# A two-block transformer kernel: eleven input panels of each layer of the second block move to split products, their rounded halves in a second ring place

## The chip, the cores and the metric

The kernel runs on one core of a Trainium2 chip. The metric is device time of one launch in microseconds (us), the median of several runs.

## The reference, cut to what matters

Two blocks of two layers each work on 256 tokens of width 1024, all in float32. The change touches only the second block, and in it the first matrix product of each layer:

```python
def second_block(x, c, ...):
    for l in range(DEPTH):                       # 2 layers
        ...
        hn = adaln(x, mix_norm_g[l], sh_m, sc_m)
        (a_q, a_k, a_v, b_qd, b_kvd, b_kr, c_q, c_k, c_v,
         c_qi, c_ki, c_wi, d_q, d_k, d_v) = jnp.split(hn @ w_in[l], IN_SPLITS, axis=-1)
        o_a = diff_attention(...)                # a_q, a_k, a_v
        o_b = latent_attention(...)              # b_qd, b_kvd, b_kr
        o_c = indexed_sparse_attention(...)      # c_*: scores of an index pick the keys
        o_d = chunk_band_attention(...)          # d_q, d_k, d_v
        y = jnp.concatenate([o_a, o_b, o_c, o_d], axis=-1) @ w_out[l]
        x = x + g_m[:, None, :] * y
        ...                                      # layer 0: a dense MLP; layer 1: 8 experts
```

## The kernel before, in words

The program is written out by hand, one instruction stream for each engine; the streams meet at semaphores. What stands first in a stream runs first, and a waiting instruction holds everything behind it on its engine.

**The ring.** All weights come through a ring of six places in on-chip memory, `ring[n % 6]`, one panel of 128x2048 floats (1 MB) in each. SyncE loads panel n when the panel that stood in its place, n-6, has been released by TensorE (`load`, L3060 in the trace). `RING_LOW`, `XT_LOW`, `GATE_HIGH`, `TAB_HIGH` and `PARTS` are not memory of their own: they lie over `ring`, `XT`, `GATE`, `TAB` and the work tiles, as another type (fp32r). So a low half is written in place, over the number that it comes from.

**Two kinds of product.** A plain panel (`panel_T` L664, `panel_tok` L675) multiplies float32 by float32, 16 matmuls, which the trace shows as 32 records. A split panel (`parted_panel`, L719) first has its weights cut in two: ScalarE copies each half of the panel as fp32r, rounded, into an area of its own (`weights_high`), VectorE subtracts it from the panel in place (`weights_low`, L2164), and TensorE forms three products for each plain one: high x high, low x high, high x low, 48 matmuls. The first block, the MLPs and the experts already work so. All 13 input panels of a layer of the second block are plain.

**A layer of the second block before its attention** (keys `s0`, `s1`; L1429 to L1471). TensorE takes panel `c_kw` (`quarters`, L736), then `c_qi`, the small `c_ki` (L1442, L743), a `take` (L634), `b_qd`, a `take`, half of the index scores of token tile 0 (L1428), `b_kvd` (160 columns wide), the other half, `a_q`, a `take` (L630, layer 0 only), half of the index scores of tile 1, `a_k`, a `take`, the other half, the transposes of the latent (L1464, L1468), `a_v`. ScalarE evacuates PSUM (L1599), applies the ReLU to the index scores (L2097) and squares the latent; VectorE sums the index scores by head (`index_sum`, L2902 and L2904) and scales the latent.

**The attention** (`paired_attention`) walks 16 units in pairs. In pass q TensorE transposes the probabilities of units 2q-4 and 2q-3 (L798), forms the scores of units 2q and 2q+1 (L812), does what is hung beside these units, and mixes the values of the two old ones (L832). Beside units 0, 1, 3, 4, 5 and 6 hang the six late panels: `LATE = {0: "d_q", 1: "d_k", 3: "d_v", 4: "c_q", 5: "c_k", 6: "c_v"}`. VectorE finds the maximum of each unit (L2246, L2250), and beside units 0, 1, 3 and 4 searches the top 64 of the index scores (L2301, L2302). ScalarE's stream for step s is, in this order: the exponential of unit s (L1685), the panels of `AHEAD` (none here), the evacuation of the late panel of unit s, and from s = 2 on the copy of the turned probabilities of unit s-2 (`turned`, L1599). GpSimd does nothing in these layers but issue four loads at the start of each.

Of the kernel before, what the change touches and what calls it, by code (L numbers as in the profile page):

```python
# [28 lines left out]
ALU = mybir.AluOpType  # L29
# [3 lines left out]
P = 128  # L33
T = 256
# [5 lines left out]
RING = 6  # L40
# [94 lines left out]
def build_program(nc, d, out):  # L135

    with ExitStack() as ctx:
# [64 lines left out]

        X_HIGH, O_HIGH, OT_LOW = [part_tile(2048 * x) for x in range(3)]
# [153 lines left out]

        weights = {}
# [20 lines left out]
        SPLIT_NORMS = ("mem", "xat0", "xat1")  # L379

# [134 lines left out]
        def part_of(n, what, c, k, i=0):  # L515
# [13 lines left out]
            return REGION_OF[u], pos, i * 16 + 16 * (pos // RING + 1), i * 12 + (made + count)  # L529
# [32 lines left out]
        LATE = {0: "d_q", 1: "d_k", 3: "d_v", 4: "c_q", 5: "c_k", 6: "c_v"}  # L562
# [12 lines left out]
        def _(pe):  # L575
# [63 lines left out]
            def panel():  # L639

                n = state["panel"]
                state["panel"] += 1
                pe.wait_ge(landed[n % RING], 16 * (n // RING + 1))
                return n, ring[n % RING]
# [37 lines left out]
            def part(name):  # L682
# [4 lines left out]
                for area in AREAS[name]:  # L687
                    held.append((area, area_holds.get(area)))
                    area_holds[area] = len(half_done)
                    half_done.append(None)  # L690
# [3 lines left out]
            def half_ready(name, half):  # L694

                n, first, held = weights[name]
                pe.wait_ge(sem("weights_low"), first + half + 1)
                return HALF[held[half][0]], RING_LOW[n % RING][:, 1024 * half:1024 * half + 1024]
# [211 lines left out]
            def late(key, s):  # L910
# [15 lines left out]
                if s in LATE:  # L926
                    name = (key, LATE[s])
                    if LATE[s][-1] == "v":
                        panel_tok(name, bank=bank)
                    else:  # L930
                        panel_T(name, bank=bank)
# [485 lines left out]
            for layer in range(2):  # L1417
# [21 lines left out]
                panel_T((k2, "c_qi"))  # L1439
# [5 lines left out]
                panel_tok((k2, "b_qd"))  # L1445
# [3 lines left out]
                panel_tok((k2, "b_kvd"), w=160)  # L1449
                index_scores(0, (2, 3))  # L1450
                panel_T((k2, "a_q"))
                if layer == 0:
                    take(16, 5)
                index_scores(1, (0, 1))
                panel_T((k2, "a_k"))
                if layer == 0:
                    take(17, 4)
                index_scores(1, (2, 3))
# [11 lines left out]
                panel_tok((k2, "a_v"), bank=7)  # L1470
# [116 lines left out]
        def moe_slot(what, it):  # L1587

            q = moe_plan["p0"] + moe_panel(what, it)
            return q % RING, 16 * (q // RING + 1)  # L1590
# [5 lines left out]
        def _(act):  # L1596
# [245 lines left out]
            def experts():  # L1842
# [73 lines left out]
                for q in range(RING):  # L1916
                    slot = (moe_plan["p0"] + q) % RING
                    act.wait_ge(landed[slot], rounds * (NE * 16 * EPANELS // RING) + 16 * ((moe_plan["p0"] + q) // RING + 1))
# [179 lines left out]

# [1141 lines left out]
```

## Time and profile before

| | us |
|---|---|
| median of 3 runs (2552.0 to 2556.07) | 2554.63 |
| the profiled execution, its own time | 2552.4 |
| its span | 2550.6 |
| TensorE busy | 2474.7 (97%) |
| VectorE busy | 1798.2 (70%) |
| ScalarE busy | 1428.3 (56%) |
| GpSimd busy | 28.7 (1%) |

Starts in the timeline are us from the start of the span. PE is TensorE's matmuls, PEld its weight loads, DVE VectorE, ACT ScalarE, POOL GpSimd, SP SyncE. "[2.72 <-ACT ...]" at a row's end is the idle time of that engine just before it and who ended it. The second block's layer 0 has its input panels and attention from 951 to 1124, layer 1 from 1331 to 1505; between them lies a dense MLP, behind them the experts.

### The profile page before, as it was taken

What the parts mean: (1) busy time and instruction counts of PE and PEld (TensorE: products, weight loads), DVE (VectorE), ACT (ScalarE), POOL (GpSimd) and SP (SyncE); (2) the same over time, 40 slices, a digit from 0 to 9 for tenths busy, and PEclk for the clock granted to TensorE, in tenths of its full rate; (3) what the DMA queues carried; (4) which work ended last, traced back from release to release, by engine and by line L of the source; (5) the groups of instructions that cost most, each with busy time, mean ns of one, the idle gap of its engine ahead of it and who ended that gap; (6) DMA issues with size and microseconds to landing.
All of it is one profiled execution on the core that took longest, in us unless ns stands there. A gap on an engine that the chain in (4) does not pass through costs nothing.

```text
span 2550.6 us, 41384 instructions
## 1 busy us (share of the span) xinstructions
PE 2474.7 (97%) x14738; PEld 2096.1 (82%) x14738; DVE 1798.2 (70%) x2631; ACT 1428.3 (56%) x2078; POOL 28.7 (1%) x41
## 2 busy tenths in 40 slices
PE   7999999998999999999999989999999999999997
PEld 7798998997889988759988757888888888888886
DVE  4654876564648763746544749898989898989897
ACT  5544544423445442444332447777778787877775
POOL 0200000000000000000000000000000000000000
PEclk9999999999999999999999999999999999999999
DMA  7554555323656555236554148898999898989897
GB/s 301 195 202 164 233 197 192 126 83 129 219 200 242 196 203 204 83 112 251 197 200 157 67 157 348 343 359 337 362 340 359 332 373 322 376 326 376 320 379 274
DMA packets 87867, 627.37 MB, mean 246 GB/s; under 512 B 9792, under 2 KB 9952, under 8 KB 13024
## 3 DMA queue, kind: packets, MB, share of 16 engines
q1 hardware_dynamic: 84512, 613.45, 63.7%
q0 software_dynamic: 2704, 11.25, 1.2%
q8 instruction: 66, 1.08, 0.2%
q10 hardware_dynamic: 560, 1.38, 0.1%
q14 instruction: 25, 0.20, 0.0%
HBM read 624.99 MB, written 1.05 MB: 245 GB/s over the span
## 4 chain that ended last, share of the span: by engine, by line
PE 91%; DVE 4%; ACT 2%; issue 1%; DMA 1%; DVEq 0%; SPq 0%; ACTq 0%
PE bank L1156 24%; PE bank L1048 13%; PE bank L1184 12%; PE bank L1062 7%; PE bank L664 7%; PE bank L719 6%; PE bank L983 6%; PE bank L675 4%; PE bank L1267 2%; PE bank L1199 1%; PE bank L1126 1%; PE bank L1171 1%; PE bank L617 1%; PE bank L832 1%; DVE sb_ringlow L2164 1%
## 5 line engine op out<-in xcount | busy, mean ns | idle before, releaser
L1599 ACT ACTIVATE sb_parts<-sb_ring 128x1024 fp32r<-128x1024 f32 x922 | 922.5, 1054 | 99.7 <-PE bank L1184 38.9
L2485 DVE TENSOR_TENSOR sb_parts<-sb_ring,sb_parts 128x1024 fp32r<-128x1024 f32 x675 | 786.4, 1217 | 9.2 <-ACT sb_parts L1599 9.2
L1156 PE MATMUL bank<-sb_parts 128*128 128x512 f32 x2688 | 661.5, 396 | 1.7 <-DVE sb_parts L2477 1.7
L1156 PEld LDWEIGHTS bank<-sb_parts 128*128 128x128 f32 x2688 | 494.9, 188 | 112.6 <-issue 8.6
L1048 PEld LDWEIGHTS bank<-sb_parts 128*128 128x128 f32 x3168 | 384.2, 192 | 9.3 <-DVE sb_parts L2388 3.7
L1048 PE MATMUL bank<-sb_parts 128*128 128x256 f32 x3168 | 386.8, 283 | 4.6 <-DVE sb_parts L2388 2.9
L1184 PE MATMUL bank<-sb_parts 128*128 128x512 f32 x1344 | 323.8, 390 | 0.0
L1184 PEld LDWEIGHTS bank<-sb_parts 128*128 128x128 f32 x1344 | 251.7, 188 | 52.0
L2388 DVE TENSOR_TENSOR sb_parts<-sb_ring,sb_parts 128x1024 fp32r<-128x1024 f32 x198 | 232.6, 1219 | 37.8 <-ACT sb_parts L1599 37.8
L1599 ACT ACTIVATE sb_REG<-bank 128x512 f32<-128x512 f32 (+3 forms) x121 | 68.8, 575 | 231.3 <-PE bank L719 60.7
L1062 PE MATMUL bank<-sb_parts 128*128 128x512 f32 x792 | 185.3, 390 | 0.0
L664 PE MATMUL bank<-sb_XT,sb_ring 128*128 128x256 f32 x768 | 170.9, 383 | 0.0
L1062 PEld LDWEIGHTS bank<-sb_parts 128*128 128x128 f32 x792 | 146.6, 188 | 29.4 <-DVE sb_parts L2388 0.3
L664 PEld LDWEIGHTS bank<-sb_XT,sb_ring 128*128 128x128 f32 x768 | 145.5, 191 | 23.0 <-issue 3.7
L1599 ACT ACTIVATE sb_parts<-bank 128x256 fp32r<-128x256 f32 (+1 forms) x142 | 59.8, 428 | 136.9 <-PE bank L1171 112.4
L2499 DVE TENSOR_TENSOR sb_parts<-bank,sb_parts 128x256 fp32r<-128x256 f32 x112 | 47.3, 423 | 76.1 <-ACT sb_parts L1599 76.1
L675 PE MATMUL bank<-sb_ring,sb_XT 128*128 128x256 f32 (+1 forms) x448 | 94.6, 369 | 1.7 <-ACT sb_XH L1599 1.7
L2427 DVE SCALAR_TENSOR_TENSOR sb_REG<-bank,sb_COL,sb_REG 128x255 f32<-128x255 f32 x88 | 42.4, 482 | 74.8 <-ACT sb_REG L1600 69.1
L1685 ACT ACTIVATE sb_REG<-sb_REG,sb_small 128x256 f32<-128x256 f32 x112 | 55.9, 500 | 65.1 <-DVE sb_small L2250 65.1
L675 PEld LDWEIGHTS bank<-sb_ring,sb_XT 128*128 128x128 f32 x448 | 80.8, 190 | 13.9 <-issue 4.6
L1600 ACT ACTIVATE sb_REG<-bank,sb_COL 128x256 f32<-128x256 f32 x92 | 38.4, 469 | 94.0 <-PE bank L1048 94.0
L1862 ACT ACTIVATE sb_REG<-bank 128x256 f32<-128x256 f32 x112 | 43.3, 387 | 78.7 <-PE bank L1156 76.8
(395 smaller groups left out, 2793.1 us busy)
## 6 DMA issues: line engine op xcount, KB each, us to landing
sb_ring<-in_moe_panels SPq DMA_DIRECT2D x342, 1024.0 KB, 4.9
sb_ring<-in_ada_w SPq DMA_DIRECT2D x48, 1024.0 KB, 5.0
sb_ring<-in_ffn_w_up SPq DMA_DIRECT2D x44, 1024.0 KB, 6.7
sb_ring<-in_ffn_w SPq DMA_DIRECT2D x33, 1024.0 KB, 6.1
sb_ring<-in_w_in SPq DMA_DIRECT2D x26, 1024.0 KB, 6.1
sb_ring<-in_ffn_w_down SPq DMA_DIRECT2D x22, 1024.0 KB, 7.4
sb_ring<-in_xattn_wkv SPq DMA_DIRECT2D x16, 1024.0 KB, 5.3
sb_ring<-in_od_w_in SPq DMA_DIRECT2D x12, 1024.0 KB, 5.0
```

The source lines that it names most:

```text
L664: m = nc.tensor.matmul(ps[:, c * T:c * T + T], wt[:, k, c * P:c * P + P], rhs[:, k, :], start=k == 0, stop=k == KD - 1)
L675: m = nc.tensor.matmul(ps[:, tb * T:tb * T + w], lhs[:, k, tb * P:tb * P + P], wt[:, k, 0:w], start=k == 0, stop=k == KD - 1)
L719: m = nc.tensor.matmul(ps[:, c * T:c * T + T], lhs, rhs, start=half == 0 and c == 0 and t == 0, stop=half == 1 and t == len(terms) - 1, sk ...
L983: m = nc.tensor.matmul(bank_in_turn(("sum", name, j))[:, :], o[:, 2 * pair + c, tb], w[:, cols], start=kk == 0 and t == 0, stop=kk == KD - ...
L1048: m = nc.tensor.matmul(banks[b][:, half * T:half * T + T], w[:, kk, :], x[:, kk, :], start=t == 0, stop=t == len(terms) - 1)
L1062: m = nc.tensor.matmul(banks[4 + j][:, :], h[:, g, tb], w[u][:, half], start=start and c == 0 and t == 0, stop=stop and c == 1 and t == 2, ...
L1156: m = nc.tensor.matmul(banks[par][:, :], x[:, k, :], w[:, cols], start=k == 0 and t == 0, stop=k == KD - 1 and t == 2, skip_group_check=True)
L1184: m = nc.tensor.matmul(banks[4 + j][:, :], h[:, par, c, :], w[:, cols], start=start and c == 0 and t == 0, stop=stop and c == 1 and t == 2 ...
L1599: return nc.scalar.activation(out, in_, ACT.Copy)
L1685: m = nc.scalar.activation(PR[:, g % 4, j, :], SS[:, g % 2, j, :], ACT.Exp, bias=NM[:, 2 * (g % 4) + j:2 * (g % 4) + j + 1], accum_out=RS[ ...
L2388: V_.tensor_tensor(as_panel(LOW[u], what), half_panel(n, what, c, it), as_panel(HIGH[u], what), ALU.subtract).then_inc(sem("low_ready"), 1)
L2485: V_.tensor_tensor(LOW[u], ring[slot][:, 1024 * c:1024 * c + 1024], HIGH[u], ALU.subtract) \
```

## The change

- `b_kvd` moves to the second place, directly behind `c_kw`; both stay plain. The index scores are spread anew between the panels that follow.
- The other eleven panels of each layer become split products (`twin_panel`): the rounded half of a panel goes to the next ring place, n+1, which is loaded with nothing (`twins`, `twin` in SyncE's stream). Each of these panels so takes two of the six places, and `landed_at` counts the loads of a place without the twins.
- ScalarE copies the input `XT` rounded into `SECOND_HIGH` (eight tiles of 128x256) and rounds each panel (`weights_high`, two copies of 128x1024). VectorE writes the input's low half in place, after `b_kvd` has been read out of it, and the low halves of `c_qi`, `b_qd`, `a_q`, `a_k`, `a_v`.
- The low halves of the six late panels are written by GpSimd (`late_low`), two subtracts of 128x1024 each. ScalarE's rounding of a late panel stands one late panel ahead, in the step of the unit before it (`AHEAD["s0"]`, `AHEAD["s1"]`), behind that step's exponential.
- Half of the gate bias of layer 1 is loaded later, behind `c_v` of layer 1, since `SECOND_HIGH` lies over its memory.

```diff
+        SECOND_HIGH = [part_tile(4096)[:, k, :] if k < 4 else GATE_HIGH[:, 1, k, :] for k in range(KD)]
...
+        LATE = {0: "d_q", 1: "d_k", 3: "d_v", 4: "c_q", 5: "c_k", 6: "c_v"}
+        for l in range(2):
+            AHEAD[f"s{l}"] = {s: (f"s{l}", LATE[t]) for s, t in zip(list(LATE), list(LATE)[1:])}
+        LATE_LOW = [(f"s{l}", x) for l in range(2) for x in LATE.values()]
...
+            def twin_panel(name, tokens=False, bank=None, fresh=None):
+
+                n, _ = part(name)
+                ps = claim(name, bank)
...
+                for half in range(2):
+                    wh, wl = half_ready(name, half)
+                    high_parts.append(wh)
+                    for c in range(2):
+                        for kk in range(4):
+                            product(wh, SECOND_HIGH, half, c, kk, start=half == 0 and c == 0 and kk == 0)
+                            product(wl, SECOND_HIGH, half, c, kk)
+                            if fresh is None:
+                                m = product(wh, low, half, c, kk, stop=half == 1 and kk == 3)
...
+                filled(m, name)
+                release(n, name)
+                release(n + 1, name)
...
-                panel_T((k2, "c_qi"))
+                panel_tok((k2, "b_kvd"), w=160)
+                twin_panel((k2, "c_qi"), fresh=layer)
...
-                panel_tok((k2, "b_qd"))
+                twin_panel((k2, "b_qd"), tokens=True)
...
             def weights_high(name):
 
                 n, _, held = weights[name]
-                act.wait_ge(landed[n % RING], 16 * (n // RING + 1))
+                act.wait_ge(landed[n % RING], landed_at(n))
+                if not held:
+                    act.wait_ge(*released[n + 1 - RING])
+                    for half in range(2):
+                        cols = slice(1024 * half, 1024 * half + 1024)
+                        copy(RING_LOW[(n + 1) % RING][:, cols], ring[n % RING][:, cols]).then_inc(sem("weights_high"), 1)
...
+                wait_drained(act, *[("norm", n, j) for j in range(4)])
+                for j in range(4):
+                    for k in (2 * j, 2 * j + 1):
+                        m = copy(SECOND_HIGH[k], XT[:, k, :])
+                    m.then_inc(sem("second_high"), 1)
                 evac((k2, "c_kw"), KP, bank_of((k2, "c_kw"))[:, :])
+                weights_high((k2, "c_qi"))
+                wait_full(act, (k2, "b_kvd"))
+                read_out(copy(KVD[:, :, :], pair_of((k2, "b_kvd"), 160)), (k2, "b_kvd"))
+                weights_high((k2, "b_qd"))
                 evac((k2, "c_qi"), QI)
+                weights_high((k2, "a_q"))
...
+                weights_low((k2, "c_qi"))
+                dve.wait_ge(sem("second_high"), 4 * layer + 4)
+                wait_full(dve, (k2, "b_kvd"))
+                for j in range(4):
+                    for k in (2 * j, 2 * j + 1):
+                        m = V_.tensor_tensor(XT_LOW[:, k, :], XT[:, k, :], SECOND_HIGH[k], ALU.subtract)
+                    m.then_inc(sem("second_low"), 1)
+                weights_low((k2, "b_qd"))
...
+                for x in LATE.values():
+                    n, first, _ = weights[f"s{layer}", x]
+                    for half in range(2):
+                        cols = slice(1024 * half, 1024 * half + 1024)
+                        pool.wait_ge(sem("weights_high"), first + half + 1)
+                        G.tensor_tensor(RING_LOW[n % RING][:, cols], ring[n % RING][:, cols],
+                                        RING_LOW[(n + 1) % RING][:, cols], ALU.subtract).then_inc(sem("late_low"), 1)
...
             for l in range(2):
-                panels(d["w_in_2"], 13 * l, 13)
+                load(d["w_in_2"][13 * l])
+                load(d["w_in_2"][13 * l + 3])
+                for i in (1, 2, *range(4, 13)):
+                    twin(d["w_in_2"][13 * l + i])
```

TensorE at the start of layer 0, before: `sb_ring` with `sb_XT` is a plain panel.

```order
L736 MATMUL bank<-sb_XT,sb_ring 32x256 x16
L664 MATMUL bank<-sb_XT,sb_ring 128x256 x16
L1442 MATMUL bank<-sb_REG,sb_CST 128x256
L743 MATMUL bank<-sb_CST,sb_REG 128x8 x2
L634 MATMUL bank<-sb_CST,sb_PARTIAL 128x1 x4
L675 MATMUL bank<-sb_ring,sb_XT 128x256 x16
```

TensorE at the same place after the change: `sb_parts` and `sb_GATEhigh` hold the rounded input, `sb_XTlow` its low half, `sb_ringlow` both halves of the weights.

```order
L790 MATMUL bank<-sb_XT,sb_ring 32x256 x16
L686 MATMUL bank<-sb_ring,sb_XT 128x160 x16
L727 MATMUL bank<-sb_parts,sb_ringlow 128x256 x16
L727 MATMUL bank<-sb_GATEhigh,sb_ringlow 128x256 x16
L727 MATMUL bank<-sb_XTlow,sb_ringlow 128x256 x16
L1494 MATMUL bank<-sb_REG,sb_CST 128x256
```

`b_kvd` has come ahead of `c_qi`, and the products of `c_qi` with the input's low half stand last in it.

ScalarE in the attention of layer 0, steps 2 to 5, before: L1685 is the pair of exponentials of one unit, `sb_REG<-bank 128x512` an evacuation or a copy of turned probabilities.

```order
L1599 ACTIVATE sb_REG<-bank 128x512
L1685 ACTIVATE sb_REG,sb_small<-sb_REG,sb_small 128x256 x2
L1599 ACTIVATE sb_REG<-bank 128x512 x2
L1685 ACTIVATE sb_REG,sb_small<-sb_REG,sb_small 128x256 x2
L1599 ACTIVATE sb_REG<-bank 128x512 x2
L1685 ACTIVATE sb_REG,sb_small<-sb_REG,sb_small 128x256 x2
```

ScalarE in the same steps after the change, from the turned probabilities of unit 0 to the rounding of `c_v`.

```order
L1650 ACTIVATE sb_REG<-bank 128x512
L1741 ACTIVATE sb_REG,sb_small<-sb_REG,sb_small 128x256 x2
L1650 ACTIVATE sb_ringlow<-sb_ring 128x1024 x2
L1650 ACTIVATE sb_REG<-bank 128x512 x2
L1741 ACTIVATE sb_REG,sb_small<-sb_REG,sb_small 128x256 x2
L1650 ACTIVATE sb_ringlow<-sb_ring 128x1024 x2
L1650 ACTIVATE sb_REG<-bank 128x512 x2
L1741 ACTIVATE sb_REG,sb_small<-sb_REG,sb_small 128x256 x2
L1650 ACTIVATE sb_ringlow<-sb_ring 128x1024 x2
```

The roundings of `c_q`, `c_k` and `c_v` (`sb_ringlow<-sb_ring`) each stand behind the exponential of the step before their own.

## Rows read from the trace of the kernel before

**Rows 1.** The page: its span, busy times, and the longest lines of the chain.

```profile
span 2550.6 us, 41384 instructions
...
PE 91%; DVE 4%; ACT 2%; issue 1%; DMA 1%; DVEq 0%; SPq 0%; ACTq 0%
```

**Rows 2.** Stages: us, busy (x instructions) of each engine, granted clock, DMA share, GB/s.

```profile
951.00:1050.00 99.00, 96.27 (x506) 79.40 (x505) 46.20 (x142) 25.93 (x66) 0.32 (x1) 1.00 0.50 186
1330.00:1430.00 100.00, 97.68 (x524) 80.57 (x522) 44.86 (x138) 26.17 (x67) 2.27 (x4) 0.99 0.44 160
```

**Rows 3.** Timeline, TensorE, layer 0: start, us, line, tiles, shape, count, idle before.

```profile
955.20 7.17 PE L664 MATMUL bank<-sb_XT,sb_ring 128*128 128x256 f32 x32
962.21 0.59 PE L1442 MATMUL bank<-sb_REG,sb_CST 128*128 128x256 f32 x2
...
972.83 4.61 PE L675 MATMUL bank<-sb_ring,sb_XT 128*128 128x160 f32 x32
...
997.21 7.07 PE L675 MATMUL bank<-sb_ring,sb_XT 128*128 128x256 f32 x32
1005.22 1.13 PE L812 MATMUL bank<-sb_REG 32*128 32x256 f32 x8 [0.94 <-issue]
1006.28 14.08 PE L664 MATMUL bank<-sb_XT,sb_ring 128*128 128x256 f32 x64
```

**Rows 4.** A split panel of block 1 (L719): stage, PE and PEld busy, clock.

```profile
598.60:604.50 5.90, 5.84 (x48) 5.77 (x48) 1.00 0.00 0
```

**Rows 5.** Making halves: ScalarE's copies, timeline; VectorE's subtract, min/median/max ns.

```profile
22.31 1.99 ACT L1599 ACTIVATE sb_parts<-sb_ring 128x1024 fp32r<-128x1024 f32 x2
...
L2164 DVE TENSOR_TENSOR sb_ringlow<-sb_ring,sb_parts x49: 1211/1218/1230, 23.9 to 711.3; 128x1024 fp32r<-128x1024 f32 x49
```

**Rows 6.** SyncE's loads at the start of layer 0, and one load's time to landing.

```profile
947.09 0.80 SPq L3060 DMA_DIRECT2D sb_ring<-in_w_in  x2
...
DMA to landing us min/median/max: 12.6/12.6/12.6
```

**Rows 7.** Timeline, pass 2 of the attention in layer 0, before `c_q`.

```profile
1034.28 1.04 PE L798 MATMUL bank<-sb_CST,sb_REG 128*128 128x128 f32 x8
1034.92 0.60 ACT L1599 ACTIVATE sb_REG<-bank 128x512 f32<-128x512 f32 x1 [7.76 <-PE bank L798]
1035.41 0.50 ACT L1685 ACTIVATE sb_REG<-sb_REG,sb_small 128x256 f32<-128x256 f32 x1
1036.31 0.48 PE L664 MATMUL bank<-sb_XT,sb_ring 128*128 128x256 f32 x1
1036.39 0.58 ACT L1599 ACTIVATE sb_REG<-bank 128x512 f32<-128x512 f32 x1
```

**Rows 8.** Timeline, pass 3 in layer 0, before `c_v`.

```profile
1051.34 1.09 PE L798 MATMUL bank<-sb_CST,sb_REG 128*128 128x128 f32 x8
1053.43 0.48 PE L675 MATMUL bank<-sb_ring,sb_XT 128*128 128x256 f32 x1
1053.52 0.58 ACT L1599 ACTIVATE sb_REG<-bank 128x512 f32<-128x512 f32 x1
```

**Rows 9.** Timeline: the last exponential of unit 0, in layer 0 and in layer 1.

```profile
1010.19 0.49 ACT L1685 ACTIVATE sb_REG<-sb_REG,sb_small 128x256 f32<-128x256 f32 x1
...
1386.57 0.49 ACT L1685 ACTIVATE sb_REG<-sb_REG,sb_small 128x256 f32<-128x256 f32 x1
```

**Rows 10.** Timeline: GpSimd's few operations in block 1, and VectorE beside them.

```profile
71.41 1.88 POOL L3012 TENSOR_TENSOR sb_REG<-sb_REG 128x1020 f32<-128x1020 f32 x1 [43.80 <-DVE sb_REG L2156]
77.56 1.07 POOL L3013 COPY sb_REG<-sb_REG 128x8 f32<-128x8 f32 x1
82.98 2.41 POOL L3019 TENSOR_TENSOR sb_REG<-sb_REG 128x1024 f32<-128x1024 f32 x1
...
83.66 2.14 DVE L2261 TENSOR_SCALAR sb_REG<-sb_REG,sb_small 128x256 f32<-128x256 f32 x2
90.19 0.62 DVE L2261 TENSOR_SCALAR sb_REG<-sb_REG,sb_small 128x256 f32<-128x256 f32 x2
```

**Rows 11.** TensorE waiting: timeline; the last row is a stage with its granted clock.

```profile
1127.88 3.51 PE L763 MATMUL bank<-sb_CST,sb_XH 128*128 128x128 f32 x16 [2.35 <-DVE sb_XH L2207]
101.41 1.09 PE L832 MATMUL bank<-sb_REG 128*64 128x128 f32 x16 [2.72 <-ACT sb_REG L1599]
...
1127.70:1131.10 3.40, 3.22 (x15) 3.25 (x16) 0.11 (x2) 1.24 (x3) 0.00 (x0) 0.50 0.03 10
```

More of the change, by code:

```diff
@@ L356, in build_program, with landed_at @@
         moe_plan = {}
+        twins = []
+        def landed_at(n):
+            return 16 * (n // RING + 1 - sum(t < n and t % RING == n % RING for t in twins))
         weights = {}
@@ L686, in part @@
                 first, held = len(half_done), []
[L687 to L690, printed above, removed]
+                LOW_ORDER[name] = sum((other in LATE_LOW) == (name in LATE_LOW) for other in LOW_ORDER)
+                if name not in AREAS:
+                    twins.append(n + 1)
+                    state["panel"] += 1
+                    half_done.extend((None, None))
+                else:
+                    for area in AREAS[name]:
+                        held.append((area, area_holds.get(area)))
+                        area_holds[area] = len(half_done)
+                        half_done.append(None)
                 weights[name] = (n, first, held)
@@ L2160, in weights_low @@
                 n, first, held = weights[name]
-                for half, (area, _) in enumerate(held):
+                for half in range(2):
                     cols = slice(1024 * half, 1024 * half + 1024)
+                    high = HALF[held[half][0]] if held else RING_LOW[(n + 1) % RING][:, cols]
                     dve.wait_ge(sem("weights_high"), first + half + 1)
-                    V_.tensor_tensor(RING_LOW[n % RING][:, cols], ring[n % RING][:, cols], HALF[area], ALU.subtract) \
+                    V_.tensor_tensor(RING_LOW[n % RING][:, cols], ring[n % RING][:, cols], high, ALU.subtract) \
                         .then_inc(sem("weights_low"), 1)
@@ L2264, in attention @@
                         late(key, s, layer)
-                    if s in AHEAD.get(key, {}):
+                    if s in AHEAD.get(key, {}) and AHEAD[key][s] not in LATE_LOW:
                         weights_low(AHEAD[key][s])
@@ L2909, in index_sum @@
                             step(m)
[L2910 removed]
+                    if heads[-1] == 7:
+                        step(V_.tensor_tensor(SC[tb], SC[tb], cst("chunked")[:, tb * T:tb * T + T], ALU.add))
                 taken(14 + 6 * layer)
+                weights_low((k2, "a_q"))
                 taken(15 + 6 * layer)
[L2914 removed]
+                index_sum(0, range(4))
                 dve.wait_ge(sem("latent_squares"), layer + 1)
@@ L2924, in _ @@
                 m.then_inc(sem("latent_normed"), 1)
+                weights_low((k2, "a_k"))
+                index_sum(0, range(4, 8))
+                weights_low((k2, "a_v"))
+                index_sum(1, range(4))
                 wait_full(dve, (k2, "kvt"))
@@ L3070, in panels, with twin @@
                     load(w[i])
+            def twin(panel):
+                load(panel)
+                assert at[0] in twins
+                at[0] += 1
             def mlp(n, gate, up, down):
```

82 lines of the change are left out of this document (49 added, 33 removed).

## The prediction, made before the changed kernel ran

> **What bounds the kernel now.** The page comes first: the chain that ended last is 91% TensorE [rows 1]. Then the stages: in the stretch that holds the input panels, TensorE is busy 96.3 of 99 us in layer 0 and 97.7 of 100 in layer 1, at full clock, while VectorE has 46 and ScalarE 26 [rows 2]. Nothing waits for weights there. So a panel that costs TensorE less shortens the kernel one for one, as long as its halves are ready; and each new wait of TensorE lengthens it one for one. Last, the timeline gives the pitch of a plain panel: `c_qi` starts at 955.20, what follows it at 962.21, so 7.0 us [rows 3].
>
> **What is removed.** A split panel of the first block has 48 matmuls in 5.84 us [rows 4]; I take 5.8 for the pitch. The difference is 7.0 - 5.8 = 1.2 us. Eleven panels in two layers make 22 x 1.2 = 26.4 us. That is the whole gain, about 1%; the rest of this part is how much of it waits take back. What is added beside TensorE: for each panel two copies of ScalarE, 1.99 us the pair, the first done after 1.05, and two subtracts of 1.22 [rows 5]. In the stretches of [rows 2] the two engines have room for that, so only the order counts.
>
> **Part 1, up to the end of `a_v`.** *Layer 0.* `c_kw` ends at 955.2; `b_kvd` (4.6 us, [rows 3]) runs until 959.8. `c_qi` is now the third load. SyncE issued the third at 947.09, and it landed 12.6 us later, at 959.7, since ada panels, the band bias and the others share the queues [rows 6]. The twin needs no load, so I leave that time. First rounded half 960.75, first low half 962.0: TensorE idles 2.2 us. The high products take 3.8, to 965.8. The input's low half is eight subtracts of 128x256; no row has them alone, and a quarter of 1.22 and half of it bound one (0.3 to 0.6, I take 0.33, nearer the quarter because operations overlap in the queue): behind the second low half (963.2) they end at 965.9, so the last 16 products end about 967.8. Before, `c_qi` ended at 962.2; with `b_kvd` put in (4.6 + 0.3 of a handoff) 967.1. This panel loses 0.7 instead of gaining 1.2. `b_qd`, `a_q`, `a_k` and `a_v` then gain 1.2 each: their loads start three panels ahead and their halves are made while TensorE does the panel before. `a_k` is the close one: its rounding stands behind the latent's squares, its low half behind the latent's scaling. I get low half 984.9 against TensorE's 985.0. One wait is new: the second pair of index scores of tile 1 now follows the first at once and needs its banks read by two ReLUs, 0.6 us. Sum: 4 x 1.2 - 0.7 - 0.6 = 3.5; with rounding of the handoffs I carry **3.1**. *Layer 1.* `c_qi` has landed early, the eight input copies delay its rounding: 0.4 us idle. Without the two `take` steps of layer 0 TensorE reaches `a_k` about 0.7 before its low half. Sum: 5 x 1.2 - 0.4 - 0.7 - 0.6 = 4.3, carried as **4.2**.
>
> **Part 2, the six late panels.** They gain 6 x 1.2 = 7.2 in each layer. Each needs in a row: the exponential of the step before, a copy of ScalarE (1.05), a subtract of GpSimd, and only then its first product. GpSimd's subtract is the unknown. The nearest rows: an add of 1020 elements took 1.88 us, a subtract of 1024, the same operation in shape, 2.41 [rows 10]. A copy of eight elements took 1.07 there when VectorE was subtracting. So 1.9 is the lower end, and 1.9 + 1.2 = 3.1, a whole VectorE subtract waited out, the upper. I take 1.9 where VectorE searches for maxima (`d_k`, `c_q`) and 2.4 where it adds biases from two inputs (`c_v`).
>
> - `d_q` is rounded before the attention: no wait.
> - `d_k` is rounded behind the exponential of unit 0. In layer 0 that ends 6.5 us after `a_v` (997.21 + 7.07 = 1004.28 against 1010.8, [rows 3, 9]); low half at 6.5 + 1.05 + 1.9 = 9.45. TensorE is ready at 2.0 + 5.8 = 7.8: **1.7** idle. In layer 1 the exponential ends at 5.15: **0.4**.
> - `d_v` is rounded in step 1 and used after the latent's products: no wait.
> - `c_q` is rounded in step 3. ScalarE can't reach that step before it has copied the turned probabilities of unit 0, and TensorE turns them only after `d_v`. In [rows 7] the turning starts at 1034.28, ScalarE is free behind the exponential at 1036.39, and TensorE starts `c_q` at 1036.31. Rounding takes until 3.2 after the turning, GpSimd until 5.2, TensorE was ready at 2.0: **3.3** with the handoffs.
> - `c_k`: rounded 8.4 after the turning, low half at 10; TensorE comes to it at 5.3 + 5.8 = 11.1: no wait, by 1 us.
> - `c_v` repeats `c_q` in the next pass: turning 1051.34, ScalarE free 1053.52, panel at 1053.43 [rows 8]: **3.7** with 2.4 for the subtract.
>
> Layer 0: 7.2 - 1.7 - 3.3 - 3.7 = -1.5. Layer 1: 7.2 - 0.4 - 3.3 - 3.7 = -0.2. The late panels together lose a little.
>
> **Sum.** Layer 0: 3.1 - 1.5 = 1.6. Layer 1: 4.2 - 0.2 = 4.0. Together 5.6 us of 26.4. The profiled execution took 2552.4, which becomes 2546.8; it stood 2.2 below the median of the three runs, so on their scale 2554.6 - 5.6 = **2549.0**. The rest is priced at nothing: the output panels still load some 40 us before use, the later gate bias has 60 us, and MLP and experts run as before on rotated ring places. In layer 1's expert loop ScalarE gets a few more register steps; ScalarE waits for TensorE there.
>
> What the clock could take back: after a wait of 2.35 us the granted clock stood at 0.50, the lower level of 1.2 GHz, for 3.4 us, and 16 transposes took 3.51; after another wait of 2.72 us the following row shows no slowing [rows 11]. So a wait of 3.3 or 3.7 costs between 0 and about 1.1 us more (2.5 us of work at half speed, the drop starting within the wait). Four such waits: 0 to 4.4. I leave it at 0 in the sum, and keep the other end for the range. The Trainium skill, "TensorE: Matmul & The Clock Gate", part 1, describes such drops after idling; nothing in the sum hangs on it.
>
> **Rivals.**
>
> *A. The late panels are hidden after all* (TensorE doesn't reach them so early, or the subtracts are quicker). With both `c_q` waits and `c_v` waits halved it gives 7 more: 2542. With no wait at all 2528, which I count as out of reach because the order of ScalarE's stream forces `c_q` and `c_v`. For it: VectorE and ScalarE have room [rows 2].
>
> *B. Clock drops and mutual blocking, mild.* All four waits cost a drop (4.4) and each of six subtracts of GpSimd is 0.3 longer: about 6 back, 2555, no change.
>
> *C. Slower.* GpSimd and VectorE hold each other up at every subtract. For it: VectorE's pair of scalings took 2.14 beside GpSimd and 0.62 without [rows 10]. If each of the 24 subtracts takes 3.1 to 3.6 instead of 1.9 to 2.4, then `d_k`, `c_q` and `c_v` wait 1.2 longer each, and `c_k` loses its 1 us of cover, because GpSimd's two halves of `c_q` end at 3.2 + 7.2 = 10.4 and the first of `c_k` only at 14: 2.0 to 2.9 more, its second half 0.7. That is 6 to 7 per layer, 13 together; with the clock's 4.4 the kernel takes 2549 + 17 = 2566. It turns slower than before from about 2.9 us per subtract with the clock drops in. The Trainium skill, "SBUF — State Buffer", section "SBUF: two separate sides", has the rule behind it: GpSimd and VectorE share a port pair that the first to start keeps for its whole instruction, against a VectorE operation with two inputs in SBUF or in a fast mode. The trace agrees (the 2.14 and the 1.07), but most of VectorE's work in these passes has one input there, which is why C is not my forecast.
>
> *D. The split panel isn't cheaper here* (halves from ring places, tokens as the stationary side): 0 gain per panel and all the waits: 2554.6 + 20 = 2575. Only the 22 panels' own rate could show it; [rows 4] speaks against it.
>
> **How the numbers follow.** Forecast, 2544 to 2554: 0.45. A: 0.17. B, 2554 to 2559: 0.25. C: 0.10. D: 0.03. A measurement of this kernel tells 0.2%, 5.1 us, from no change. Faster than that: three fifths of the forecast's share and all of A, together 0.45 or a little more, 0.47. Slower: C and D, 0.13. The rest, 0.40, is within 0.2%. The range from 2540 to 2559 leaves out the far part of A and C and D.
>
> **What would show it.** Right: 48 matmuls in 5.8 us in each of the 22 panels; TensorE idle 3 to 4 us before `c_q` and before `c_v` in both layers, with a GpSimd subtract as the one that ends it; 2 us before `c_qi` in layer 0; GpSimd busy some 24 x 2 = 48 us more. Wrong: waits elsewhere (`a_k`, `c_k`), a granted clock of 0.5 within the two attentions, subtracts of GpSimd over 2.9 us, or a longer MLP or expert stage.

## The result, and the profile after

| | before | after |
|---|---|---|
| median, us (18 runs each) | 2554.61 (2552.0 to 2558.19) | 2560.64 (2556.84 to 2565.03) |
| the profiled execution, its own time | 2552.4 | 2557.38 |
| its span | 2550.6 | 2555.5 |

The ratio is 1.0022, 95% interval 1.0015 to 1.0029: the changed kernel is 6.0 us slower, where 5.6 faster was forecast. The time lies above the range, by 1.6 us.

The page of the changed kernel (span, busy time by engine, chain), which answers to [rows 1]:

```profile
span 2555.5 us, 42296 instructions
...
PE 2458.1 (96%) x15090; PEld 2097.1 (82%) x15090; DVE 1859.9 (73%) x2667; ACT 1474.2 (58%) x2138; POOL 85.8 (3%) x65
...
PE 89%; DVE 5%; ACT 3%; issue 1%; DMA 1%; POOL 0%; DVEq 0%; SPq 0%; ACTq 0%
```

TensorE is busy 16.6 us less than before (2474.7) and the kernel is still longer, so it waits more. How much more, and what else, two stages show, one for each layer. The first begins at the end of the transposes ahead of `c_kw`, the second just ahead of those transposes; both end at the wait before the last matmuls of the output product, at the same place of the program before and after. First before, then after: window, length, busy time (instructions) of PE, PEld, DVE, ACT, POOL, then the granted clock.

```profile
952.15:1115.70 163.55, 158.08 (x904) 120.39 (x904) 82.04 (x228) 58.50 (x157) 0.00 (x0) 1.00 0.37 136
1327.95:1493.31 165.36, 159.54 (x912) 122.06 (x912) 81.70 (x226) 58.07 (x156) 2.75 (x4) 0.99 0.35 127
```

```profile
952.31:1122.16 169.85, 151.88 (x1081) 123.35 (x1080) 112.52 (x246) 81.21 (x187) 28.52 (x12) 0.95 0.36 131
1333.54:1498.07 164.53, 148.86 (x1089) 120.61 (x1088) 112.12 (x244) 80.92 (x186) 31.93 (x17) 0.98 0.37 131
```

The two stages together grew by 334.38 - 328.91 = 5.5 us, against 4.9 between the two spans, so the whole difference is here. Length less PE busy is TensorE's idle time: 11.3 before, 33.6 after, 22.3 more. PE busy fell by 16.9 only, and the granted clock by 0.05 in layer 0 and 0.01 in layer 1. Next, who ended TensorE's waits, in layer 0 and in layer 1 (sum, times, longest):

```profile
PE bank L727 <- POOL sb_ringlow L3130: 9.4, 3, 3.6
PE bank L727 <- DVE sb_ringlow L2232: 2.8, 1, 2.8
...
PE bank L727 <- POOL sb_ringlow L3130: 8.1, 3, 3.6
PE bank L978 <- ACT sb_XH L1650: 1.3, 1, 1.3
```

L727 is the split product, L3130 GpSimd's subtract, L978 the latent's products. The three waits for GpSimd of each layer stand before `d_k`, `c_q` and `c_v`: 2.15, 3.62, 3.63, and in layer 1 0.83, 3.63, 3.62. The wait before `c_q` and what released it, in time order, answers to [rows 7]:

```profile
1034.27 1.99 ACT L1650 ACTIVATE sb_ringlow<-sb_ring 128x1024 fp32r<-128x1024 f32 x2
1035.38 4.68 POOL L3130 TENSOR_TENSOR sb_ringlow<-sb_ring,sb_ringlow 128x1024 fp32r<-128x1024 f32 x2 [15.86 <-ACT sb_ringlow L1650]
1037.87 0.55 PE L727 MATMUL bank<-sb_parts,sb_ringlow 128*128 128x256 f32 x1 [3.62 <-POOL sb_ringlow L3130]
```

What the prediction left out of its sum is the next view: the five stretches in the two attentions in which the granted clock stood at 0.50 (1.2 GHz). Before, there was none between the first unit and the end of either attention.

```profile
1012.79:1016.20 3.41, 3.41 (x18) 3.41 (x17) 3.31 (x8) 2.85 (x6) 2.84 (x2) 0.50 0.37 156
1036.68:1043.50 6.82, 5.63 (x26) 5.66 (x27) 6.72 (x7) 3.41 (x8) 6.82 (x4) 0.50 0.00 0
1057.16:1063.99 6.83, 5.22 (x24) 5.25 (x25) 6.83 (x5) 1.94 (x6) 3.84 (x2) 0.50 0.24 100
1415.56:1418.97 3.41, 3.38 (x16) 3.41 (x17) 3.41 (x2) 2.24 (x4) 3.41 (x2) 0.50 0.00 0
1436.04:1439.45 3.41, 3.41 (x19) 3.41 (x18) 3.41 (x3) 0.00 (x0) 1.69 (x1) 0.50 0.00 0
```

Each begins near the end of one of the waits above (1012.0, 1037.9, 1058.8, 1415.6, 1435.5) and reaches into the panel behind it: of 23.9 us, TensorE worked 21.1 at half speed. Of these six waits only the one of 0.83 has none. The 2.76 before `c_qi`, where all is at full clock behind it, is the exception.

The drops are not a matter of this one execution. The clock granted over the whole span lies between 0.988 and 0.992 in all 18 runs of the changed kernel, and between 0.994 and 0.997 in the 38 runs of before that stood beside the experiments.

### The profile page after: what moved, and what is told of

It is laid out like the page before. It is cut to its first block, busy times and chain, and to the rows that moved or that the text cites. A ratio compares the mean times of both kernels' runs of the same rounds, so it can differ in the third digit from the quotient of the medians.

```text
span 2555.5 us, 42296 instructions
## 1 busy us (share of the span) xinstructions
PE 2458.1 (96%) x15090; PEld 2097.1 (82%) x15090; DVE 1859.9 (73%) x2667; ACT 1474.2 (58%) x2138; POOL 85.8 (3%) x65
## 4 chain that ended last, share of the span: by engine, by line
PE 89%; DVE 5%; ACT 3%; issue 1%; DMA 1%; POOL 0%; DVEq 0%; SPq 0%; ACTq 0%
PE bank L1207 24%; PE bank L1099 13%; PE bank L1235 12%; PE bank L1113 7%; PE bank L773 6%; PE bank L1034 6%; PE bank L727 5%; PE bank L675 3%; PE bank L1318 2%; PE bank L686 1%; PE bank L1250 1%; PE bank L1177 1%; PE bank L1222 1%; PE bank L628 1%; DVE sb_ringlow L2232 1%
## 5 line engine op out<-in xcount | busy, mean ns | idle before, releaser
L1667 ACT ACTIVATE sb_XH<-sb_H 128x1024 f32<-128x1024 f32 x24 | 25.3, 1055 | 105.4 <-DVE sb_H L2426 58.2
L2232 DVE TENSOR_TENSOR sb_ringlow<-sb_ring,sb_TABhigh 128x1024 fp32r<-128x1024 f32 x43 | 51.5, 1226 | 47.1 <-ACT sb_TABhigh L1650 46.9
L2232 DVE TENSOR_TENSOR sb_ringlow<-sb_ring,sb_parts 128x1024 fp32r<-128x1024 f32 x49 | 57.9, 1220 | 20.4 <-ACT sb_parts L1650 20.4
L675 PE MATMUL bank<-sb_XT,sb_ring 128*128 128x256 f32 x320 | 70.3, 380 | 0.0
```

Of the source, the lines that this page charges most:

```text
L675: m = nc.tensor.matmul(ps[:, c * T:c * T + T], wt[:, k, c * P:c * P + P], rhs[:, k, :], start=k == 0, stop=k == KD - 1)
L2232: V_.tensor_tensor(RING_LOW[n % RING][:, cols], ring[n % RING][:, cols], high, ALU.subtract) \
```

## The experiments

**Theory 1**: the waits cost what they last and, on top, the drops of the clock behind them, some 9 us in all; without the drops the forecast would have stood nearly right. **Rivals**: the loss comes from Part 1 (the five early panels); from GpSimd as such, so that VectorE would do the low halves better; or the drops have nothing to do with the waits.

All ran with the kernel before beside them on the same chip. The first four share one set of its runs (2554.25), the next four another (2553.02), the last has its own (2554.1). The changed kernel did not run beside them; its 2560.64 stands against 2554.61 for before.

### 1. The waits filled with work

In the changed kernel TensorE multiplies the input's rounded half by itself into the panel's own bank, which the panel then overwrites.

```diff
 ps = claim(name, bank)
...
+for _ in range({"c_q": 24, "c_v": 24, "d_k": 14 if name[0] == "s0" else 0}.get(name[1], 0)):
+    nc.tensor.matmul(ps[:, 0:T], SECOND_HIGH[0][:, 0:P], SECOND_HIGH[1], start=True, stop=True,
+                     skip_group_check=True)
```

> Adds idle work alone: 24 matmuls of 128x256 into the claimed bank before the products of c_q and c_v, 14 before d_k of layer 0 (about 3 us and 1.7 us of TensorE, inside waits of 3.6 and 2.2 us); the products overwrite them, so the result is unchanged. Theory 1 (the granted clock falls in or behind these waits and takes back some 11 us): the five drops within the two attentions of the changed kernel, 23.9 us at 0.50, vanish or shrink to one or two, the waits for GpSimd stay as they are, and the kernel is 6 to 11 us faster than the changed one, 2550 to 2555 us. Rival (the clock is a bystander, and the lost time lies in the waits and in engines holding each other up): no change or slower, 2560 to 2563 us, since nothing that TensorE waits for comes sooner.

Measured: 2551.82, ratio 0.9993 (0.9984 to 1.0002). 110 matmuls more, and the kernel is 9 us faster than the changed one. The two stretches in which the clock had been low, by the same view:

```profile
1036.50:1043.40 6.90, 6.37 (x52) 6.06 (x51) 6.59 (x6) 6.03 (x12) 5.59 (x3) 1.00 0.32 132
1057.00:1063.80 6.80, 6.28 (x53) 6.08 (x52) 6.80 (x5) 1.99 (x7) 3.97 (x2) 1.00 0.23 98
```

TensorE is busy 6.4 us with 52 matmuls instead of 5.6 with 26, at full clock; part of the 52 are the added ones. No stretch at 0.50 is left in either attention; one stands at 964.8, behind the wait before `c_qi` (2.22 here). The panels can't start earlier than their low halves, so it is the clock that gave nearly all of the 9 us. In the two profiled executions the stages are 7.4 apart (334.4 against 327.0), 0.5 of it by the shorter wait before `c_qi`.

### 2. Each rounding a step earlier

```diff
-            AHEAD[f"s{l}"] = {s: (f"s{l}", LATE[t]) for s, t in zip(list(LATE), list(LATE)[1:])}
+            AHEAD[f"s{l}"] = {s: (f"s{l}", LATE[t]) for s, t in zip(range(5), list(LATE)[1:])}
```

`c_q`, `c_k` and `c_v` are so rounded in steps 2, 3 and 4.

> ScalarE's roundings of c_q, c_k and c_v are moved one step ahead, to steps 2, 3 and 4, in front of the copy of the turned probabilities that holds ScalarE; nothing else. Both theories: the waits of 3.6 us before c_q and c_v vanish in both layers (14.5 us). Theory 1: the drops behind them vanish too (four of five), another 8 to 10 us, 2560.6 - 24 = 2537 us (2535 to 2540). Rival: only the waits, 2560.6 - 14.5 = 2546 us, with the drops still there or without a price.

Measured: 2546.21, ratio 0.9969 (0.9957 to 0.9981); 14 us better than the changed kernel, but 9 short of the 2537 of a kernel rid of all these waits and their drops. The waits before `c_q` and `c_v` are gone; `d_k` keeps its own, and a new one stands before the latent's products, since the rounding of `c_q` now stands ahead of their evacuation on ScalarE (layer 0, then layer 1):

```profile
PE bank L978 <- ACT sb_XH L1650: 2.2, 1, 2.2
PE bank L727 <- POOL sb_ringlow L3130: 2.2, 1, 2.2
...
PE bank L978 <- ACT sb_XH L1650: 3.2, 1, 3.2
```

Two drops of 3.4 us are left, both in layer 0.

### 3. Part 1 alone

Only the five early panels of a layer are split. The late ones are plain as before and multiply the residual instead of the input, because the input's place now holds its low half.

```diff
-twin_panel(name, tokens=LATE[s][-1] == "v", bank=bank)
+if LATE[s][-1] == "v":
+    panel_tok(name, lhs=HX, bank=bank)
+else:
+    panel_T(name, rhs=HX, bank=bank)
```

> Part 1 alone: c_qi, b_qd, a_q, a_k, a_v as split products, the six late panels plain float32 again, of the residual instead of the normed input (which is overwritten in place by then), so the result is wrong and the work of the same size. From the two traces part 1 gains 2.5 us in layer 0 and 6.1 in layer 1: 2554.6 - 8.6 = 2546 us, and no drop of the clock within the attentions. If part 1 were the one that costs, it would stand at 2555 or above.

Measured: 2547.58, ratio 0.9977 (0.9968 to 0.9986), 6.7 faster than before: Part 1 is a gain, as forecast (7.3). No drop stands in either attention. The rival that puts the loss there falls.

### 4. VectorE makes the late low halves

```diff
-LATE_LOW = [(f"s{l}", x) for l in range(2) for x in LATE.values()]
+LATE_LOW = []
...
+                weights_low((k2, "d_q"))
...
-                        G.tensor_tensor(RING_LOW[n % RING][:, cols], ring[n % RING][:, cols],
-                                        RING_LOW[(n + 1) % RING][:, cols], ALU.subtract).then_inc(sem("late_low"), 1)
```

> The late panels' low halves by VectorE (1.22 us each instead of GpSimd's 2.40), in its own order behind the search of the step; nothing else. Theory 1: each of the four long waits shrinks by 1.2 us or so, to 2.4, and the drops of the clock become fewer or shorter: 2560.6 - 5 - 2 to 8 = 2548 to 2554 us. If GpSimd's blocking of VectorE were the cause, the same gain would come with the drops unchanged. If VectorE's own queue is late (its search stands in front), waits grow instead: 2560 or above.

Measured: 2564.47, ratio 1.0044 (1.003 to 1.0058), 4 slower than the changed kernel. VectorE takes 1.22 for a subtract that GpSimd does in 2.40, and the waits before `c_q` and `c_v` did shrink as expected, from 3.6 to 2.46 in both layers. Others took more than that back (layer 0, then layer 1):

```profile
PE bank L727 <- DVE sb_ringlow L2232: 11.7, 5, 2.6
PE bank L978 <- ACT sb_XH L1650: 1.6, 1, 1.6
...
PE bank L727 <- DVE sb_ringlow L2232: 9.6, 4, 3.4
PE bank L978 <- ACT sb_XH L1650: 3.1, 1, 3.1
```

The first line holds the 2.30 before `c_qi` too. The waits before `d_k` are 0.5 longer (2.64 and 1.32), `c_k`, which had none, waits 1.85 and 3.37, and the latent's products 1.58 and 3.12. Before `c_k` the subtract follows VectorE's search for the top 64 without a pause; before `c_q` VectorE itself had stood 3.19 us, until ScalarE had rounded the panel:

```profile
1038.43 1.22 DVE L2232 TENSOR_TENSOR sb_ringlow<-sb_ring,sb_ringlow 128x1024 fp32r<-128x1024 f32 x1 [3.19 <-ACT sb_ringlow L1650]
...
1047.73 1.23 DVE L2232 TENSOR_TENSOR sb_ringlow<-sb_ring,sb_ringlow 128x1024 fp32r<-128x1024 f32 x1
```

The stages are 4.2 longer than those of the changed kernel at the same PE busy (300.7). So a faster subtract helps where ScalarE's rounding comes last, and the order of VectorE's stream takes it back elsewhere.

### 5 and 6. The bare price of a wait, in the kernel before

Nothing of the change is in these two. GpSimd does six subtracts of 192 elements one after the other, from the end of the exponential of step 3 and of step 5, and TensorE waits for them before `c_q` and `c_v`. The loop with the matmuls, seven plain ones in each of the four waits, is in the second kernel alone.

```diff
 ps, wt = claim(name, bank), cols_of(slot)
+for _ in range(7 if name[1] in ("c_q", "c_v") and name[0] in ("s0", "s1") else 0):
+    nc.tensor.matmul(ps[:, 0:T], XT[:, 0, 0:P], XT[:, 1, :], start=True, stop=True, skip_group_check=True)
+if name[1] in ("c_q", "c_v") and name[0] in ("s0", "s1"):
+    pe.wait_ge(sem("idle"), 12 * int(name[0][1]) + (6 if name[1] == "c_q" else 12))
```

> The kernel before the change, nothing of the change in it, with a wait of TensorE put ahead of c_q and of c_v in both layers: GpSimd does six small subtracts of 192 elements, one after the other (about 3 to 4 us), from the end of the exponential that TensorE's path reaches at that moment, into columns that hold zeros (constants less themselves), and TensorE waits for them. The bare price of a wait of that length. With waits of 3.0 to 3.7 and nothing else lost the kernel takes 12 to 15 us more, about 2568. By the theory that each such wait brings a drop to 0.50 which costs another 1.7 to 3.4 us, it takes 7 to 13 more than that: about 2577, with the drops behind the four waits in the rows.

> The kernel of e7_before_waits with seven plain matmuls of 128x256 (about 3.1 us) that TensorE does into the panel's own bank ahead of each of the four waits, so that the path is as long and TensorE is busy most of it. By the theory the drops go and only the waits' length is left: about 2568. If a drop doesn't depend on TensorE's idleness, it takes what e7_before_waits takes.

Measured: 2584.51 with idle waits (ratio 1.0121, 1.0106 to 1.0137) and 2577.44 with filled ones (1.0094, 1.0078 to 1.0109): the work makes it 7.1 faster. Both are above what was expected, since the waits before `c_v` came out longer than meant. The idle kernel's waits, of one layer (the other is alike), and its two stages:

```profile
PE bank L679 <- POOL sb_WN L3050: 5.8, 1, 5.8
PE bank L666 <- POOL sb_WN L3050: 3.8, 1, 3.8
...
952.83:1130.14 177.31, 162.39 (x905) 123.44 (x904) 83.94 (x228) 58.56 (x157) 8.00 (x12) 0.97 0.34 126
1343.71:1523.69 179.98, 164.21 (x913) 125.50 (x912) 83.64 (x226) 58.12 (x156) 10.78 (x16) 0.95 0.33 116
```

The stages of the filled one:

```profile
956.83:1129.78 172.95, 164.68 (x932) 125.54 (x932) 83.96 (x228) 58.51 (x157) 7.99 (x12) 1.00 0.35 129
1340.94:1515.64 174.70, 166.07 (x940) 127.07 (x940) 83.66 (x226) 58.06 (x156) 10.77 (x16) 0.99 0.34 120
```

Idle: the stages grew by 28.4, of which 19.4 is idle time and 9.0 is PE busy, for one record more in each stage. That 9.0 is the clock alone, 2.2 for each of four waits; in its four low stretches behind them TensorE worked 17.9 us, half of which is the same 9.0. Filled: they grew by 18.7, the length of the waits. So the clock's price needs no split panels and no ring places; four bare waits bring it, and work in them takes it away. Outside the two stages the profiled executions are 2.7 and 4.8 longer than that of before, and low stretches there account for about that: the idle kernel has two more (half of their 6.8 us of work is 3.4), the filled one a long one with 12.8 us of work in it, and lacks that of [rows 11] with 3.2 (half of the difference is 4.8).

```profile
101.45:104.86 3.41, 3.41 (x13) 2.59 (x9) 0.96 (x2) 2.81 (x5) 0.00 (x0) 0.50 0.47 195
1152.76:1156.17 3.41, 3.41 (x18) 3.41 (x18) 1.82 (x2) 0.00 (x0) 0.00 (x0) 0.50 0.53 135
...
611.80:625.45 13.65, 12.80 (x41) 7.75 (x40) 5.83 (x8) 4.05 (x6) 0.00 (x0) 0.50 0.00 0
```

At 101 and at 611 the program is that of before, so the clock also falls where nothing was changed.

### 7 and 8. No late panel rounded on the path, and the loads behind `c_qi`

```diff
-            AHEAD[f"s{l}"] = {s: (f"s{l}", LATE[t]) for s, t in zip(list(LATE), list(LATE)[1:])}
+            AHEAD[f"s{l}"] = {s: (f"s{l}", LATE[t]) for s, t in zip(range(1, 5), list(LATE)[2:])}
...
                         beside_units(key, s)
+                        if behind:
+                            weights_high(AHEAD[key][s])
...
+                weights_high((k2, "d_k"))
...
+                pool.wait_ge(sem("weights_high"), weights[f"s{layer}", "c_qi"][1] + 1)
```

`d_k` is rounded behind the exponential of the lambdas, ahead of the attention; `c_q` in step 2, behind the latent's evacuations (`behind` is true in that step). The last line is in the eighth kernel alone, on GpSimd, ahead of the band bias and the latent's weights.

> The changed kernel with each late panel rounded before TensorE's path can reach it: d_k behind the exponential of the lambdas, ahead of the attention; c_q in step 2, behind the evacuations of the latent's products; c_k in step 3, c_v in step 4. Theory (a wait costs its length and a drop of the granted clock after it): the waits before d_k (2.15 and 0.83), c_q and c_v (3.6 each) go, the one before the evacuations of the latent that rounding a step earlier had made (2.17 and 3.19) goes too, and no drop to 0.50 is left in the attentions; against 2546.2 of the kernel with only the roundings a step earlier this is 3.0 + 5.4 of waits and 3.4 of two drops: about 2534.5. Rival 1 (the clock's losses come from something else than these waits): the drops stay, about 2538. Rival 2 (rounding is put before something else on ScalarE's stream that TensorE then waits for): some 5 us of new waits at another line, 2540 or more.

> The kernel of e5_all_earlier in which GpSimd issues the band bias and the latent's weights only when the first half of c_qi is rounded, so that the load of c_qi shares the queues with fewer others. If the wait of 2.76 before c_qi in layer 0 comes from the landing beside these loads, it shrinks to about 0.5 and the kernel gains 2 us more, about 2532.5. Rival: the load lands late because it is issued late, the wait stays and nothing changes; or the latent's weights now land after TensorE wants them, and it is slower by their wait.

Measured: 2540.98, ratio 0.9954 (0.994 to 0.9967), then 2536.96, ratio 0.993 (0.9917 to 0.9944). All waits on GpSimd are gone. The second edit gave 4 where 2 were expected, and the wait before `c_qi` in layer 0, 2.4 in the seventh kernel, disappears, so the landing beside GpSimd's loads had made it. Its stage is 2.7 shorter for it (158.76, then 156.07); where the rest of the 4 lies isn't shown, the two profiled executions being only 0.8 apart. But the first missed its 2534.5 by 6.5: the wait before the latent's products stayed, now 3.64 and 2.36. Its cause is in the streams of ScalarE and VectorE (the eighth kernel, layer 0):

```profile
1020.93 0.51 ACT L1741 ACTIVATE sb_REG<-sb_REG,sb_small 128x256 f32<-128x256 f32 x1 [5.33 <-DVE sb_small L2322]
...
1016.58 2.54 DVE L2376 TENSOR_TENSOR sb_OT<-sb_OT 128x256 f32<-128x256 f32 x1
1019.15 0.29 DVE L2377 TENSOR_SCALAR sb_REG<-sb_OT 128x256 f32<-128x256 f32 x1
1019.48 0.69 DVE L2318 SCALAR_TENSOR_TENSOR sb_REG<-bank,sb_TAB 128x512 f32<-128x512 f32 x1
```

ScalarE stood 5.3 us before the exponential of unit 2, because VectorE came to its bias add (L2318) only after the search for the top 64; the evacuation that TensorE waited for stood behind that exponential. Of these 5.3 some 2.1 are the comparison L2376, which took 2.54 beside a GpSimd subtract, and 0.42 in experiment 4 without one.

### 9. The latent's evacuation ahead of the exponential of unit 2

```diff
+if key[0] == "s" and s == LATENT_AT:
+    for tb in range(NT):
+        evac((key, "uq", tb), QB[:, tb, :, :],
+             bank_of((key, "uq", tb))[:, 0:384].rearrange("p (h n) -> p h n", h=4))
 if s < len(us):
     exponentials(key, s)
```

> The kernel of e6_loads_later in which ScalarE copies the latent's query products out of their two banks ahead of the exponential of unit 2 instead of behind it. In e6_loads_later TensorE waited 3.64 and 2.36 before the next products into these banks, while ScalarE waited 5.3 for a bias add that VectorE did behind its search for maxima, and each wait was followed by 3.4 us at 0.50. If only this order made them, the waits shrink to about 0.8 each and both drops go: 2.8 + 1.5 + 2 x 1.7 = 7.7 less, about 2529. If the exponential of unit 2 binds TensorE next (turning it, two units later), half comes back: about 2533. Rival: VectorE's search is the bound of the pass and the wait only moves to another line: 2537.

Measured: 2530.25 (2528.92 to 2533.64), ratio 0.9906 (0.9889 to 0.9922), against 2529 expected. It beats both kernels, by 24 us the one before. Its stages:

```profile
953.69:1107.73 154.04, 146.32 (x1081) 118.37 (x1080) 109.58 (x246) 81.40 (x187) 31.51 (x16) 0.99 0.41 144
1319.53:1471.97 152.44, 145.23 (x1088) 117.55 (x1088) 108.33 (x244) 81.13 (x186) 32.09 (x17) 1.00 0.40 141
```

They are 22.4 us shorter than before; idle time is 14.9 against 11.3. One part did not come as expected: the waits at the latent's products did not shrink to 0.8, they are gone, but the panel behind them now waits 2.66 and 1.35, and one low stretch stays. Nearly the whole gain of the change, 24 of 26.4 us, was there to be had; the order of three other streams kept it from TensorE.

## Why the prediction was wrong

Kernels with all 22 panels split have the same matmuls, so their PE busy differs by the clock alone (a record can be missing):

| kernel | layer 0: PE busy, us at 0.50 | layer 1: PE busy, us at 0.50 |
|---|---|---|
| changed | 151.88, 17.1 | 148.86, 6.8 |
| each rounding a step earlier | 148.45, 6.8 | 145.79, none |
| all earlier (7) | 146.85, 3.4 | 148.47, 6.8 |
| latent first (9) | 146.32, 3.4 | 145.23, none |

With no low stretch a stage has some 145.3 us of matmuls. The changed kernel has 6.6 and 3.6 more, 10.2 in all; before had one low stretch at the start of layer 1, with 3.1 us of work in it, worth some 1.5. So the sum of the two stages, against the steps of the prediction:

| term | predicted | measured |
|---|---|---|
| split products instead of plain | -26.4 | -25.6 (2 x 145.3 against 2 x 158.1) |
| idle time of TensorE, all waits | +20.8 | +22.3 |
| clock | 0 (at most +4.4) | +8.7 |
| sum | -5.6 | +5.4 |

- **What bounds the kernel; 1.2 us per panel**: right. Measured 1.16.
- **Part 1**: `a_v` ends at 1001.99 where it had ended at 1004.28, 2.5 earlier after the end of `c_kw`, predicted 3.1. The wait before `c_qi` was 2.8 for 2.2. In layer 1 it gained 6.1 for 4.2: 0.9 of that came before the end of `c_kw`, where the low stretch of before fell away, and the expected waits before `c_qi` (0.4) and `a_k` (0.7) were not there. Together 8.6 for 7.3.
- **The three waits**: right. `d_k` 2.15 and 0.83 (1.7 and 0.4), `c_q` 3.62 and 3.63 (3.3), `c_v` 3.63 and 3.62 (3.7), `d_q`, `d_v`, `c_k` none for GpSimd. One was missed: the latent's products in layer 1 wait 1.25, where before had 0.3.
- **GpSimd's subtract**: 2.40 everywhere, beside searches and beside adds. The 1.9 was 0.5 too low for `d_k` and `c_q`, which is their excess. The row of the same shape and operation, 2.41 [rows 10], was the right one. Rival C's 3.1 to 3.6 didn't come, though not for the reason given against it: VectorE's scalings, with one input, were held up as well (see the last section); the subtracts were not.
- **The clock, the step that failed**: "So a wait of 3.3 or 3.7 costs between 0 and about 1.1 us more ... I leave it at 0 in the sum". Two things were wrong in it. The choice: 0 rested on one row, the 2.72 after which nothing was slow, against another, the 2.35 with its drop. That row was one execution's luck: in the trace of the changed kernel the same 2.72, at the same place of the first block, has a low stretch behind it, and eight matmuls take 3.68 where they had taken 1.99 (first before, then after).

```profile
102.44 1.99 PE L1253 MATMUL bank<-sb_REG 128*128 128x256 f32 x8
...
100.37 1.09 PE L886 MATMUL bank<-sb_REG 128*64 128x128 f32 x16 [2.72 <-ACT sb_REG L1650]
101.40 3.68 PE L1304 MATMUL bank<-sb_REG 128*128 128x256 f32 x8
...
101.43:104.84 3.41, 3.41 (x11) 2.78 (x9) 1.15 (x3) 2.81 (x5) 0.00 (x0) 0.50 0.59 245
```

And the size: 1.1 allowed for 2.5 us of work at half speed, the rest of the stretch falling into the wait, while the row itself has 3.22 us of work in its 3.40. Here three stretches lasted 3.4 and two 6.8, with TensorE at work in 21.1 of 23.9 us, and a stretch of 3.4 costs 1.7 when it is full. Five stretches cost some 10, and four in the kernel before 9.0. The waits before `d_k` and `c_qi` in layer 0, 1.7 and 2.2 by the prediction's own sum, had no such price at all, since it counted only the four of 3.3 and 3.7; `d_k` brought the fifth stretch.

- **Rival B** had the mechanism (clock drops at the waits), at half the size, and was given 0.25. It was the right case to forecast, with 2 per wait.
- **Late panels**: predicted to lose 1.7 in both layers; from the end of `a_v` to the end of the stage layer 0 lost 8.8 and layer 1 5.2, 14.0 in all. Most of the 12.3 us of difference, some 10, is the clock.

The Trainium skill, "TensorE: Matmul & The Clock Gate", part 1, has the time lost as the length of the low stretch times one half, which gives 11.9 for the 23.9 us above. The rows show 10.2, nearer to half of the 21.1 us in which TensorE worked: the part of a stretch that falls into a wait costs nothing.

Had each of the four waits been priced at one full stretch of 3.4 us, the sum would have been 6.8 more, 2556, and within the range.

## What to carry to other kernels

Price a wait of 3.5 us or more on a busy TensorE at its length plus a low-clock stretch behind it at half speed (here 2.0 to 2.2 us for each), not at nothing because one row shows no drop: the same wait can have one in the next execution. When a change adds a producer (a rounding, a subtract) to an engine's stream, put it where the stream has already passed, and then look for what that placement delays; here each of three moves uncovered the next wait. A few throwaway matmuls into a bank that is about to be overwritten tell in one run whether the clock is part of a loss.

## What the runs showed of the hardware that was not expected

**GpSimd's subtracts kept their time beside VectorE; VectorE's operations did not.** All 24 subtracts took nearly the same time, while VectorE's operations with two inputs in SBUF (on-chip memory), and its scalings of SBUF tiles, stretched. First GpSimd in the changed kernel; then VectorE between 996 and 1070 there (line, operation, tiles, count, busy, mean ns), then the same two groups in the kernel of experiment 4, where GpSimd does nothing.

```profile
L3130 POOL TENSOR_TENSOR sb_ringlow<-sb_ring,sb_ringlow x24: 2342/2396/2543, 998.3 to 1435.3; 128x1024 fp32r<-128x1024 f32 x24
...
L2329 DVE TENSOR_SCALAR sb_REG<-sb_REG,sb_small 128x256 f32<-128x256 f32 x14 | 13.6, 1014 | 0.2
L2980 DVE SCALAR_TENSOR_TENSOR sb_OT<-sb_O,sb_WI,sb_OT 128x256 f32<-128x256 f32 x5 | 4.5, 907 | 0.1
L2314 DVE SCALAR_TENSOR_TENSOR sb_REG<-bank,sb_TAB 128x512 f32<-128x512 f32 x8 | 5.5, 689 | 8.5 <-PE bank L866 8.4
```

```profile
L2329 DVE TENSOR_SCALAR sb_REG<-sb_REG,sb_small 128x256 f32<-128x256 f32 x12 | 3.7, 350 | 0.2
L2980 DVE SCALAR_TENSOR_TENSOR sb_OT<-sb_O,sb_WI,sb_OT 128x256 f32<-128x256 f32 x7 | 3.4, 485 | 0.2
```

On average 350 became 1014 ns and 485 became 907; the bias add, which reads PSUM and one SBUF tile, kept its 689. The stages tell the sum: VectorE is busy 112.5 us with GpSimd's subtracts and 110.1 with twelve subtracts of its own in their place (12 x 1.22 = 14.6), so GpSimd's 28.5 us cost VectorE some 17. Here VectorE had room for most of it; the comparison of experiment 8 is where it reached the path. The Trainium skill, "SBUF — State Buffer", section "SBUF: two separate sides", says that the one that starts first holds the shared ports for its whole instruction and the other is blocked. VectorE's side of it agrees: in the changed kernel a scaling that began at 1037.79, 0.1 us behind a subtract of 2.38, took 2.43. GpSimd's side shows in the first block, where its copy of eight elements took 0.19 us, and 1.07 [rows 10] when it began 0.4 us behind a VectorE subtract:

```profile
76.51 0.19 POOL L3013 COPY sb_REG<-sb_REG 128x8 f32<-128x8 f32 x1
...
77.14 2.58 DVE L2164 TENSOR_TENSOR sb_ringlow<-sb_ring,sb_TABhigh 128x1024 fp32r<-128x1024 f32 x2 [0.54 <-ACT sb_TABhigh L1599]
```

In the late panels GpSimd was the one with the long instructions, two or four in a row, and none took more than 2.54.

**The same wait brings a drop in one execution and none in another.** The 2.72 of [rows 11] stands in all eleven traces at a place where their programs are alike; in five it has a low stretch behind it (the changed kernel, experiments 1, 2, 5 and 8), in six none. The 2.35 behind layer 0 has one in seven of eleven. Of all 43 waits of TensorE from 2.1 to 3.2 us in these traces, 24 have a stretch that begins in them or at most 1.5 us behind; of the eleven from 3.4 to 5.8 us, all have one. The length of the stretch, 3.4 or 6.8 us, does not follow the wait either: 3.62 and 3.63 before `c_q` brought 6.8 in one layer and 3.4 in the other. And 13.7 us at 0.50 in experiment 6 have no wait of even 1 us just ahead of them.
